# A two-layer hybrid decoder trunk on one core: mixer outputs and differential q and k turned on VectorE instead of TensorE, and weight high halves begun earlier

## The chip, the core and the metric

The kernel runs on one core of a Trainium2 chip. The core has TensorE (PE), VectorE (DVE), ScalarE (ACT), GpSimd (POOL) and SyncE (SP), each with its own queue of instructions, and DMA queues. SBUF is the core's memory of 128 partitions, PSUM holds matmul outputs in banks of 128 x 512 float32. The metric is the device time of one execution in microseconds (us).

## The reference

x (512 tokens x 2048, float32) goes through two layers:

```python
h = rms_norm(x, norm_g)
p = h @ w_in                       # 2048 x 7192: all projections at once
ya = gla_mixer(aq, ak, av, alr, ...)  * silu(az)      # gated linear attention
yb = swa_mixer(bq, bk, bv, ...)       * silu(bz)      # sliding window 128, sinks
yc = diff_mixer(cq, ck, cv, ...)      * silu(cz)      # differential attention
yd = gdn_mixer(dqkv, dbeta, da, ...)  * silu(dz)      # gated DeltaNet
x  = x + concat([ya, yb, yc, yd]) @ w_out             # 2048 x 2048
```

Each mixer has 4 heads, each 128 wide. In the differential mixer a head's q and k are two halves of 64 columns; each half is normalised over its 64 columns and scaled by its gain (q also by 64 ** -0.5), two softmaxes over all earlier tokens are taken, and w = p1 - lambda * p2 is applied to v.

## The kernel before, in words

**Projections.** To keep float32 accuracy, every operand of a projection is split into a high half (rounded by the engine to the matmul's format) and a low half (the rest), and each product is three matmuls: hi x hi, hi x lo, lo x hi, in `project` (line 552). A projection step ("kt") takes 128 input rows to 512 columns: 4 PSUM banks x 3 = 12 matmuls of 128 x 512. A layer has 14 chunks of 512 output columns (dq, dk, dv, dz, bz, az, aq, av, bq, bkv, cq, ck, cv, cz) x 16 steps, and the output projection of 4 x 12 + 4 x 4 steps: 288 steps, in 144 pairs of weights. The first 12 input rows of the output projection are the outputs of DeltaNet (chunks 0 to 3 of `y`), linear attention (4 to 7) and the window mixer (8 to 11); the last four steps of each output group wait for the differential mixer (12 to 15), which runs during the first 12.

**Weights.** SyncE loads each pair of weight steps raw (`w_raw`, 3 buffers). GpSimd issues a second load of the same pair into `w_hi` (3 buffers, line 484, `high_halves`), which arrives rounded, and makes `w_lo = w_raw - w_hi` (4 buffers, line 509), two subtractions a pair. It issues the load of pair g + 1 after the first subtraction of pair g; the issue waits until TensorE has used up pair g - 2. `kt_done` counts TensorE's steps.

**Mixers beside projections.** Each mixer is a generator of stages for TensorE; `project` hands one out after so many matmuls (its `stages`, `skip`, `spread`). The order on each engine is written out by hand, with counted semaphores (`Steps`) between engines. DeltaNet runs beside dz, bz, az, aq, av; linear attention tiles 0 to 3 beside bq, bkv, cq, ck; the window tiles 0 and 1 beside cv and 2 and 3 beside cz; the differential tiles 3, 2, 1, 0 beside the four output groups. All four mixers share the four PSUM banks `mix`.

**What the change touches.** The window tile `swa` has, between its scores (line 797) and the transposes of its probabilities (818), 8 transposes (807) that turn the differential q and k of that tile, normalised on VectorE (1886), into `mix`; ScalarE copies them back with their gains (1366). `turn_y` (953) turns each mixer's output, four 128 x 128 transposes a chunk: chunks 0 to 3 in front of the last step of cz, chunks 4 to 11 in pairs in front of the first four steps of the first output group, chunks 12 to 15 near the end. From `mix`, ScalarE makes the high half (`y_hi`, 1383) and VectorE the low half (`y_lo`, 1928). The scores of the differential mixer are at 843 (tiles 3 and 2) and 875 (tiles 1 and 0, two heads at once). In the linear attention VectorE turns q and k in blocks of 32 (1835, 1840), then waits for TensorE, copies under a mask (1844) and updates the state (1852, 1855), for which TensorE's output matmuls (749) wait. ScalarE asks for the residual (4 MB, line 1391) when the last window tile is done. `x_group` makes the low halves of the next layer's input and the sums of its squares, with `x_sums` (936, 938) on TensorE in front of the last step of dq; `lambda_sums` and `lambdas` prepare parameters.

Of the kernel before, what the change touches and what calls it, by code (L numbers as in the profile page):

```python
# [7 lines left out]
F32 = mybir.dt.float32  # L8
# [7 lines left out]
P = 128  # L16
# [3 lines left out]
GW = 512  # L20
# [27 lines left out]
SLOT = dict(dq=4, dk=5, dv=8, dz=3, bz=4, az=5, aq=6, av=7, bq=8, bkv=9, cq=10, ck=11, cv=12, cz=13)  # L48
# [118 lines left out]
PREP_PE = "q k".split()  # L167
PREP_ACT = "qT kT".split()
# [46 lines left out]
def hybrid_trunk(nc, x, wstream, wsmall, pcol, prow, wlr, cf, masks, out, rows):  # L215
    ctx = ExitStack()
    with ctx:
# [68 lines left out]
        def cols(ap, n=128, parts=P):  # L286
# [35 lines left out]
              for i in range(2)]  # L322
# [12 lines left out]
                 PT=s7[:, 1024:2048].rearrange("p (h c) -> p h c", h=HEADS))  # L335
        RQ = general[:, :, :].rearrange("p a (g c) -> p (a g) c", c=DK)
        f3 = [slot(3)[:, i] for i in range(4)]
        Z = dict(S=((f3[0], f3[1]), (f3[2], f3[3])), WT=(unit(4, 0), unit(4, 1)), OS=unit(4, 2), SQO=unit(4, 3),
                 GATE=unit(5, 0))
# [3 lines left out]
        cden = stat[:, 52:60]  # L343
        ssb, rsb = stat[:, 64:70], stat[:, 72:78]
# [14 lines left out]
        rows_out, rows_in = sem("rows_out"), sem("rows_in")  # L359
        kt_done = sem("kt_done")  # L360
        acc_ready, acc_free = sem("acc_ready"), sem("acc_free")
        xres_in, xout = sem("xres_in"), sem("xout")
        lam_steps = sem("lam_steps")
        lam_act = sem("lam_act")
# [21 lines left out]
        def lay(prefix, *parts):  # L386
# [4 lines left out]
        X_DVE = Steps(sem("x_dve"), [s for n in T for s in [f"lo{4*n+i}" for i in range(4)] + [f"pair{n}"] +  # L391
                                     ([f"four{n}"] if n else []) + [f"g{n}"]])
        S_PE = Steps(sem("setup_pe"), ["rsum", "small", "ba", "dec"] + [f"yT{k}" for k in range(KT)])
# [19 lines left out]
        R_PE = Steps(sem("prep_pe"), names("", T, PREP_PE))  # L413
        R_ACT = Steps(sem("prep_act"), names("", T, PREP_ACT))
# [44 lines left out]
        def _(pool):  # L459
# [27 lines left out]
            for l in range(DEPTH):  # L487
                for i in range(PAIRS):
# [5 lines left out]

                    pool.wait_ge(raw_in[g % RAW], g // RAW * 16 + 16)
                    if g >= FIRST_HI:
                        pool.wait_ge(hi_in[g % HI], len(range(FIRST_HI + (g - FIRST_HI) % HI, g + 1, HI)) * 16)
                    for k in range(2):
# [12 lines left out]
                        if k == 0 and FIRST_HI <= g + 1 < DEPTH * PAIRS:  # L511
                            high_halves(g + 1)
# [3 lines left out]
        def _(pe):  # L516
# [244 lines left out]
            def swa(l, t):  # L761
# [50 lines left out]
                pe.wait_ge(R_ACT.sem, R_ACT.at(l, f"{t}.kT"))  # L812
# [14 lines left out]
            def dif(l, t):  # L827

                n = t + 1
                qT, kT, v = (slot(SLOT[c]) for c in ("cq", "ck", "cv"))  # L830

                def scores(h):
# [33 lines left out]
                def pair_scores(g):  # L866
# [5 lines left out]
                    for h in (2 * g, 2 * g + 1):  # L872
                        for m in range(2):
                            r = slice(DK * m, DK * m + DK)
                            last = nc.tensor.matmul(mix[m][:, 256 * (h % 2):256 * (h % 2) + P * n],  # L875
                                                    qT[r, t, HD * h:HD * h + HD], kT[r, 0:n, HD * h:HD * h + HD],
# [64 lines left out]
            def turn_y(l, k):  # L941

                src = slot(SLOT[("dz", "az", "bz", "cz")[k // 4]])
                if k == 0:

                    pe.wait_ge(B_DVE.sem, B_DVE.at(l, f"{TILES-1}.y3"))
                    pe.wait_ge(R_ACT.sem, R_ACT.at(l, f"{TILES-1}.kT"))
                elif k == 3 * HEADS:
                    pe.wait_ge(C_DVE.sem, C_DVE.at(l, "0.y3"))
                elif k >= 4:  # L950
                    pe.wait_ge(S_DVE.sem, S_DVE.at(l, f"ylo{k-4}"))
# [5 lines left out]
            for l in range(DEPTH):  # L957
# [50 lines left out]
                for i in range(2):  # L1008
# [3 lines left out]
                    def y_first(k, l=l):  # L1012
# [1107 lines left out]
```

## Time and profile before

| | |
|---|---|
| median of 3 runs (lowest, highest) | 1816.85 us (1816.59, 1820.76) |
| the profiled execution: its time, its span | 1817.91 us, 1816.1 us |
| granted clock of TensorE | 1.0 of full speed |
| TensorE busy | 1806.1 us, 99% |
| GpSimd, VectorE, ScalarE busy | 920.1, 854.8, 505.0 us |
| DMA | 324.99 MB, mean 179 GB/s |
| w_raw, w_hi loads of 512 KB, issue to landing (median) | 4.5 us, 3.8 us |
| TensorE's waits by name, whole span | w_lo 2.6 us, issue 1.2, others 3.0 |

A matmul's recorded duration is longer than its step: matmuls follow each other before the one in front has drained, so their durations overlap, and TensorE's cost of something is read from the distance between starts. A group of instructions of one line is merged to one row with a count. "Idle" in brackets is the time in which the engine had nothing in flight before that instruction, and who ended it. Fp32 matmuls that aren't transposes have two records each.

### The profile page before, as it was taken

Reading aid. Unit: us, or ns where it says so; the run is one execution under the profiler, and the core shown is the slowest. Engines: PE = TensorE matmul, PEld = TensorE weight load, DVE = VectorE, ACT = ScalarE, POOL = GpSimd, SP = SyncE. Lnnn points to the kernel's source line nnn. Section 1 sums busy time; section 2 is a strip of 40 time slices with the busy share of each in tenths; the row PEclk is TensorE's granted clock in tenths of the full one; section 3 lists DMA queues with packets and bytes.
Section 4 is the critical chain, followed back from the end, with each engine's and each line's share of the span. In section 5 each row is a group of like instructions: output and inputs, shape, how many; then the busy total and the mean of one; then the engine's idle time right before and its main releaser. Section 6 shows DMA issues by size and latency. Waiting matters only on the chain. (4 is left out here: it accounts for less than half of the span.)

```text
span 1816.1 us, 23463 instructions
## 1 busy us (share of the span) xinstructions
PE 1806.1 (99%) x9382; PEld 1484.4 (82%) x9382; DVE 854.8 (47%) x1829; ACT 505.0 (28%) x967; POOL 920.1 (51%) x864
## 2 busy tenths in 40 slices
PE   9999999999999999999999999999999999999999
PEld 7788888888888888788877888888888878877887
DVE  7546815523333443544534478264333344445342
ACT  6213114022222543322312131141222235433220
POOL 5555544545555444445465555445455454444454
PEclk9999999999999999999999999999999999999999
DMA  7566545645555547456765665555555565474556
GB/s 273 169 186 208 175 152 160 186 143 183 177 175 181 163 140 243 129 161 185 233 213 181 191 203 176 158 155 171 162 178 177 169 184 156 148 242 134 160 170 209
DMA packets 94508, 324.99 MB, mean 179 GB/s; under 512 B 10144, under 2 KB 10688, under 8 KB 94144
## 3 DMA queue, kind: packets, MB, share of 16 engines
q1 hardware_dynamic: 43904, 155.73, 27.8%
q0 software_dynamic: 40320, 146.82, 26.7%
q10 hardware_dynamic: 10176, 20.94, 3.2%
q8 instruction: 74, 1.21, 0.3%
q14 instruction: 34, 0.28, 0.0%
HBM read 315.05 MB, written 8.40 MB: 178 GB/s over the span
## 5 line engine op out<-in xcount | busy, mean ns | idle before, releaser
L509 POOL TENSOR_TENSOR w_lo<-w_raw,w_hi 128x512 fp32r<-128x512 f32 x575 | 759.5, 1321 | 650.3 <-DMA w_hi<-in_wstream 488.4
L552 PE MATMUL acc<-w_hi,actT_hi 128*128 128x512 f32 x1408 | 559.8, 398 | 0.0
L552 PE MATMUL acc<-w_hi,actT_lo 128*128 128x512 f32 x1408 | 548.9, 390 | 0.0
L552 PE MATMUL acc<-w_lo,actT_hi 128*128 128x512 f32 x1408 | 548.5, 390 | 0.0
L552 PE MATMUL acc<-actT_hi,w_hi 128*128 128x512 f32 x896 | 358.4, 400 | 4.3 <-POOL w_lo L509 2.6
L552 PE MATMUL acc<-actT_hi,w_lo 128*128 128x512 f32 x896 | 349.6, 390 | 0.0
L552 PE MATMUL acc<-actT_lo,w_hi 128*128 128x512 f32 x896 | 349.2, 390 | 0.0
L552 PEld LDWEIGHTS acc<-w_hi,actT_lo 128*128 128x128 f32 x1408 | 264.3, 188 | 55.9
L552 PEld LDWEIGHTS acc<-w_hi,actT_hi 128*128 128x128 f32 x1408 | 264.5, 188 | 55.1 <-issue 2.8
L552 PEld LDWEIGHTS acc<-w_lo,actT_hi 128*128 128x128 f32 x1408 | 264.7, 188 | 51.7
L484 POOL DMA_DIRECT2D w_hi<-in_wstream x280 | 159.8, 571 | 234.6 <-PE acc L552 230.3
L552 PEld LDWEIGHTS acc<-actT_hi,w_hi 128*128 128x128 f32 x896 | 168.3, 188 | 54.1 <-issue 19.8
L552 PEld LDWEIGHTS acc<-actT_hi,w_lo 128*128 128x128 f32 x896 | 168.2, 188 | 35.9
L552 PEld LDWEIGHTS acc<-actT_lo,w_hi 128*128 128x128 f32 x896 | 168.5, 188 | 32.7 <-issue 0.5
L1579 DVE SCALAR_TENSOR_TENSOR slots<-slots,pcol_all 128x511 f32<-128x511 f32 (+2 forms) x72 | 86.6, 1208 | 1.7
L1052 ACT ACTIVATE slots<-acc,xr 128x512 f32<-128x512 f32 x56 | 37.9, 690 | 167.8 <-PE acc L552 167.8
L1937 DVE TENSOR_TENSOR slots<-acc,slots 128x512 f32<-128x512 f32 x64 | 43.1, 690 | 88.0 <-PE acc L552 88.0
L1560 DVE TENSOR_TENSOR slots<-acc,slots 128x512 f32<-128x512 f32 x24 | 15.7, 689 | 129.0 <-PE acc L552 91.8
L1818 DVE SCALAR_TENSOR_TENSOR slots<-mix,slots 128x256 f32<-128x256 f32 x8 | 3.4, 425 | 133.3 <-ACT slots L1294 133.3
L601 PEld LDWEIGHTS mix<-slots 128*128 128x128 f32 x400 | 48.5, 191 | 2.0
L601 PE MATMUL mix<-slots 128*128 128x128 f32 x400 | 49.0, 275 | 0.0
L1928 DVE SCALAR_TENSOR_TENSOR actT_lo<-mix,pcol_all,actT_hi 128x512 fp32r<-128x512 f32 x32 | 22.4, 746 | 42.1 <-ACT actT_hi L1383 42.1
(264 smaller groups left out, 1586.2 us busy)
## 6 DMA issues: line engine op xcount, KB each, us to landing
w_raw<-in_wstream SPq DMA_DIRECT2D x288, 512.0 KB, 4.5
w_hi<-in_wstream POOLq DMA_DIRECT2D x280, 512.0 KB, 3.8
out_x<-slots ACTq DMA_DIRECT2D x7, 1024.0 KB, 7.1
slots<-in_x ACTq DMA_DIRECT2D x1, 4096.0 KB, 19.5
slots<-out_x ACTq DMA_DIRECT2D x1, 4096.0 KB, 19.2
slots<-in_x SPq DMA_DIRECT2D x3, 1024.0 KB, 12.0
slots<-rows ACTq DMA_DIRECT2D x2, 1024.0 KB, 5.7
out_x<-slots ACTq DMA_DIRECT2D x4, 256.0 KB, 2.1
```

Source lines behind the costliest of these rows:

```text
L484: pool.dma_start(w_hi[:, g % HI].rearrange("p a n -> p (a n)"), wstream[g:g + 1].rearrange("a p n -> p (a n)")).then_inc(hi_in[g % HI], 16)
L509: pool.tensor_tensor(w_lo[:, n % RING], w_raw[:, g % RAW, k], w_hi[:, g % HI, k].bitcast(F32), ALU.subtract).then_inc(w_ready, 1)
L552: last = nc.tensor.matmul(acc[b][:, :], lhsT, rhs, start=(k == 0 and i == 0), stop=(k == kts - 1 and i == 2))
L601: last = nc.tensor.matmul(mh[bank][:, h], lhsT[:, h], rhs[:, h], start=True, stop=True)
L1052: nc.scalar.activation(slot(SLOT[c])[:, b], acc[b][:, :], ACT.Copy, scale=r) \
L1560: dve.tensor_tensor(slot(SLOT[c])[:, b], acc[b][:, :], rrow, ALU.mult).then_inc(acc_free, 1)
L1579: dve.scalar_tensor_tensor(dst[:, d:], src[:, 0:SEQ - d], tap[i], dst[:, d:], ALU.mult, ALU.add).then_inc(CONV_DVE.sem, CONV_DVE.one(f"{c} ...
L1818: dve.scalar_tensor_tensor(V["G"], mix[1][:, 0:256], 0.0, V["T0"], ALU.min, ALU.subtract) \
L1928: dve.scalar_tensor_tensor(actT_lo[:, k], mix[k % 4][:, :], pcv(l, PC["y"] + k), actT_hi[:, k].bitcast(F32), ALU.mult, ALU.subtract) \
L1937: dve.tensor_tensor(xs, acc[b][:, :], xs, ALU.add).then_inc(acc_free, 1)
```

## The change

Mixer outputs: the outputs of DeltaNet (dz) and linear attention (az) are turned into slots of their own on VectorE, in blocks of 32 x 32 (`turn_blocks`, 16 instructions each), dz during the linear attention's tiles 0 and 1, az during the window tiles. `turn_y` keeps chunks 8 to 15; 8 to 11 are turned together in front of the third step of the first output group. `y_hi` and `y_lo` of chunks 0 to 7 read the turned slots.

Differential q and k: VectorE turns each tile's q and k within the four blocks of 32 partitions (`turn_c`, 8 instructions a tile), ScalarE's queue writes the four pieces to DRAM and reads them back with the blocks in their places (`hop_back`, 8 DMAs a tile), and ScalarE scales q once for all (gain of q x gain of k x 64 ** -0.5). The scores read q with a column step of 4 numbers and k in runs of 32.

Weights: in the first 8 and the last 8 pairs of a layer GpSimd issues the next pair's high halves before it waits for this pair's.

Order: the residual is asked for after cz is taken out of PSUM; the input's low halves 12 to 15 come before the third sum of squares; the taps are halved first of all, and the lambda sums come after the convolution of dq in layer 0; the differential scores' buffer is slot 10 in place of 3, cq is in slot 3, cz in 5.

```diff
-SLOT = dict(dq=4, dk=5, dv=8, dz=3, bz=4, az=5, aq=6, av=7, bq=8, bkv=9, cq=10, ck=11, cv=12, cz=13)
+SLOT = dict(dq=4, dk=5, dv=8, dz=3, bz=4, az=5, aq=6, av=7, bq=8, bkv=9, cq=3, ck=11, cv=12, cz=5)
+Y_TURNED = dict(dz=10, az=13)
...
+        turned_piece = dict(q0=smT[:, 0:256], q1=smT[:, 256:512], k0=wlr_sb[:, :], k1=s6[:, 768:1024])
...
@@ GpSimd, for each pair i of a layer (g over both layers)
+                    follows = FIRST_HI <= g + 1 < DEPTH * PAIRS
+                    dense_only = i < KT // 2 or i >= PAIRS - LAST_KTS // 2
+                    if follows and dense_only:
+                        high_halves(g + 1)
                     pool.wait_ge(raw_in[g % RAW], g // RAW * 16 + 16)
...
-                        if k == 0 and FIRST_HI <= g + 1 < DEPTH * PAIRS:
+                        if k == 0 and follows and not dense_only:
                             high_halves(g + 1)
@@ TensorE, sliding-window tile
-                pe.wait_ge(N_DVE.sem, N_DVE.at(l, f"{t}.ck"))
-                for i, c in enumerate(("cq", "ck")):
-                    for h in H:
-                        last = nc.tensor.transpose(mh[i][:, h], slot(SLOT[c])[:, t, h * HD:h * HD + HD], ident)
-                    last.then_inc(R_PE.sem, R_PE.one(f"{t}.{'qk'[i]}"))
                 yield
                 yield
-                pe.wait_ge(R_ACT.sem, R_ACT.at(l, f"{t}.kT"))
+                pe.wait_ge(B_ACT.sem, B_ACT.at(l, f"{t}.kT"))
@@ TensorE, differential scores (the paired scores of tiles 1 and 0 alike)
+                qT = slot(SLOT["cq"]).rearrange("p t (c h) -> p t h c", h=HEADS)
+                kT = slot(SLOT["ck"]).rearrange("p t (b h c) -> p t b h c", b=P // BLK, h=HEADS)
...
                         pe.wait_ge(S_DVE.sem, S_DVE.at(l, f"ylo{3*HEADS-1}"))
+                        pe.wait_ge(hop_in, 128 * TILES * (l + 1))
+                        pe.wait_ge(Q_ACT.sem, Q_ACT.at(l, f"q{TILES-1}"))
...
-                        last = nc.tensor.matmul(mix[m][:, 0:P * n], qT[r, t, HD * h:HD * h + HD],
-                                                kT[r, 0:n, HD * h:HD * h + HD], start=True, stop=True)
+                        last = nc.tensor.matmul(mix[m][:, 0:P * n], qT[r, t, h],
+                                                kT[r, 0:n, :, h].rearrange("p t b c -> p (t b) c"),
+                                                start=True, stop=True)
@@ TensorE, outputs turned
-                    def y_first(k, l=l):
-                        if k == KT - 1:
-                            for m in range(4):
-                                turn_y(l, m)
...
-                            for m in (4 + 2 * k, 5 + 2 * k):
-                                if m < 3 * HEADS:
+                            if k == 2:
+                                for m in range(2 * HEADS, 3 * HEADS):
                                     turn_y(l, m)
@@ ScalarE
+                    if CHUNKS[8 + t] == "cq":
+                        act.wait_ge(Y_DVE.sem, Y_DVE.at(l, f"dz{P//BLK-1}{P//BLK-1}"))
                     take_out(l, CHUNKS[8 + t])
...
+                def hop_back(t):
+                    act.wait_ge(hop_out, 64 * (TILES * l + t + 1))
+                    for i, c in enumerate(("cq", "ck")):
+                        for r in range(P // BLK):
+                            act.dma_start(slot(SLOT[c])[BLK * r:BLK * r + BLK, t].rearrange("p (b c) -> p b c", b=P // BLK),
+                                          hops[l, i, :, t, P * r:P * r + P].rearrange("(b p) c -> p b c", b=P // BLK)) \
+                                .then_inc(hop_in, 16)
...
+                    if t:
+                        hop_back(t - 1)
+                    for i, p in enumerate(TURNED):
+                        act.wait_ge(T_DVE.sem, T_DVE.at(l, f"{t}.{p}"))
+                        act.dma_start(hops[l, i // 2, :, t, 256 * (i % 2):256 * (i % 2) + 256], turned_piece[p]) \
+                            .then_inc(hop_out, 16)
                     w(B_DVE, "nm")
...
-                    for i, c in enumerate(("q", "k")):
-                        w(R_PE, c)
-                        g = PC[f"g{c}_c"]
-                        nc.scalar.activation(slot(SLOT["c" + c])[:, t], mix[i][:, :], ACT.Copy,
-                                             scale=pcv(l, g)).then_inc(R_ACT.sem, R_ACT.one(f"{t}.{c}T"))
...
+                hop_back(TILES - 1)
+                for k in range(2 * HEADS):
+                    y_hi(k)
+                take_out(l, "cz")
                 act.wait_ge(B_DVE.sem, B_DVE.at(l, f"{TILES-1}.y3"))
...
                 act.dma_start(xT, (out if l else x).rearrange("(k p) n -> p k n", p=P)).then_inc(xres_in, 16)
-                for k in range(4):
-                    y_hi(k)
-                take_out(l, "cz")
-                for k in range(4, 12):
-                    y_hi(k)
+                act.wait_ge(hop_in, 128 * TILES * (l + 1))
+                for t in T:
+                    nc.scalar.activation(slot(SLOT["cq"])[:, t], slot(SLOT["cq"])[:, t], ACT.Copy,
+                                         scale=pcv(l, PC["gq_c"])).then_inc(Q_ACT.sem, Q_ACT.one(f"q{t}"))
+                for k in range(2 * HEADS, 3 * HEADS):
+                    y_hi(k)
@@ VectorE
+                def turn_blocks(c, rows):
+                    src = slot(SLOT[c]).rearrange("p t (h c) -> p t h c", h=HEADS)
+                    dst = slot(Y_TURNED[c]).rearrange("p h (t c) -> p t h c", t=TILES)
+                    for r in rows:
+                        rs_ = slice(BLK * r, BLK * r + BLK)
+                        for f in range(P // BLK):
+                            fs = slice(BLK * f, BLK * f + BLK)
+                            dve.transpose(dst[fs, :, :, rs_], src[rs_, :, :, fs]) \
+                                .then_inc(Y_DVE.sem, Y_DVE.one(f"{c}{r}{f}"))
...
+                    if t < 2:
+                        turn_blocks("dz", [2 * t])
                     w(A_PE, "a")
...
                     gate(A_DVE, l, t, gz, V["GATE"])
+                    if t < 2:
+                        turn_blocks("dz", [2 * t + 1])
...
+                def turn_c(t, pieces):
+                    for p in pieces:
+                        i = TURNED.index(p)
+                        c, half_ = ("cq", "ck")[i // 2], 2 * (i % 2)
+                        v = slot(SLOT[c])[:, t].rearrange("p (h r c) -> p h r c", h=HEADS, r=P // BLK)
...
+                        if TILES * l + t:
+                            dve.wait_ge(hop_out, 64 * (TILES * l + t))
+                        for r in range(2):
+                            o = turned_piece[p][:, P * r:P * r + P].rearrange(
+                                "p (h c) -> p h c" if c == "ck" else "p (c h) -> p h c", h=HEADS)
+                            last = dve.transpose(o, v[:, :, half_ + r])
+                        last.then_inc(T_DVE.sem, T_DVE.one(f"{t}.{p}"))
                 sums(0)
                 normalise(0)
+                turn_c(0, TURNED[:2])
                 for t in T:
...
+                    turn_c(t, TURNED[2:])
...
                     gate(B_DVE, l, t, gz, W["GATE"])
+                    turn_blocks("az", [t])
...
                         normalise(t + 1)
+                        turn_c(t + 1, TURNED[:2])
+                    if t == TILES - 1:
+                        for k in range(HEADS):
+                            y_lo(k)
                     w(B_PE, "pv")
...
-                for k in range(12):
+                dve.wait_ge(hop_out, 64 * TILES * (l + 1))
+                dve.memset(smT[:, :], 1.0).then_inc(ones_done, 1)
+                for k in range(HEADS, 3 * HEADS):
                     y_lo(k)
```

## Rows read from the trace of the kernel before

**Rows 1.** Page, busy time of each engine, share of the span, instructions.

```profile
PE 1806.1 (99%) x9382; PEld 1484.4 (82%) x9382; DVE 854.8 (47%) x1829; ACT 505.0 (28%) x967; POOL 920.1 (51%) x864
```

**Rows 2.** Timeline of TensorE (start, duration, group, count), around a window tile's transposes.

```profile
603.81 0.39 PE L552 MATMUL acc<-w_hi,actT_lo 128*128 128x512 f32 x1
...
605.85 0.40 PE L552 MATMUL acc<-w_hi,actT_lo 128*128 128x512 f32 x1
606.08 1.04 PE L807 MATMUL mix<-cf_sb,slots 128*128 128x128 f32 x8
606.88 0.47 PE L552 MATMUL acc<-w_hi,actT_hi 128*128 128x512 f32 x1
607.19 0.39 PE L552 MATMUL acc<-w_lo,actT_hi 128*128 128x512 f32 x1
```

**Rows 3.** TensorE's groups by form (busy us, mean ns, idle before): both transpose lines.

```profile
L953 PE MATMUL mix<-cf_sb,slots 128*128 128x128 f32 x128 | 16.3, 272 | 0.0
...
L807 PE MATMUL mix<-cf_sb,slots 128*128 128x128 f32 x64 | 8.3, 272 | 0.0
```

**Rows 4.** Timeline of TensorE in front of the last input step.

```profile
695.53 0.40 PE L552 MATMUL acc<-w_hi,actT_lo 128*128 128x512 f32 x1
...
697.75 0.39 PE L552 MATMUL acc<-w_lo,actT_hi 128*128 128x512 f32 x1
```

**Rows 5.** Timeline of TensorE at the layer boundary, matmuls that waited (idle in brackets).

```profile
908.43 0.47 PE L552 MATMUL acc<-actT_hi,w_hi 128*128 128x512 f32 x1 [0.66 <-issue]
...
915.13 0.47 PE L552 MATMUL acc<-actT_hi,w_hi 128*128 128x512 f32 x1 [1.01 <-POOL w_lo L509]
...
922.43 0.47 PE L552 MATMUL acc<-actT_hi,w_hi 128*128 128x512 f32 x1 [1.58 <-POOL w_lo L509]
```

**Rows 6.** Timeline of GpSimd at the layer boundary.

```profile
908.27 0.57 POOL L484 DMA_DIRECT2D w_hi<-in_wstream  x1
...
913.41 1.57 POOL L509 TENSOR_TENSOR w_lo<-w_raw,w_hi 128x512 fp32r<-128x512 f32 x1 [3.24 <-issue]
```

**Rows 7.** Busy us by engine, clock, DMA share, GB/s, 910 to 920 us.

```profile
910.00:920.00 10.00, 8.99 (x40) 7.12 (x39) 9.93 (x12) 4.94 (x8) 3.96 (x5) 1.00 0.95 342
```

**Rows 8.** VectorE's groups by form: two turns in blocks of 32.

```profile
L1835 DVE STREAM_TRANSPOSE slots<-slots 32x128 f32<-32x128 f32 x128 | 38.7, 303 | 4.0
...
L1758 DVE STREAM_TRANSPOSE slots<-slots 32x256 f32<-32x256 f32 x16 | 7.0, 436 | 0.5
```

**Rows 9.** Busy us by engine, 624 to 644 us (window tiles).

```profile
624.00:644.00 20.00, 20.00 (x105) 16.98 (x104) 10.00 (x18) 10.54 (x23) 9.53 (x9) 1.00 0.54 163
```

**Rows 10.** Timelines of ScalarE, TensorE and GpSimd, window tiles and after.

```profile
629.61 1.24 ACT L1366 ACTIVATE slots<-mix,pcol_all 128x512 f32<-128x512 f32 x2
...
633.44 1.03 PE L818 MATMUL mix<-cf_sb,slots 128*128 128x128 f32 x8
...
681.45 0.60 ACT L1371 ACTIVATE slots<-mix 128x512 f32<-128x512 f32 x1 [2.39 <-PE mix L818]
...
703.75 1.28 POOL L509 TENSOR_TENSOR w_lo<-w_raw,w_hi 128x512 fp32r<-128x512 f32 x1 [8.35 <-DMA w_hi<-in_wstream]
```

**Rows 11.** Timeline of ScalarE's queue, a DMA issue.

```profile
9.80 0.52 ACTq L1125 DMA_DIRECT2D slots<-in_prow  x1
```

**Rows 12.** Timelines of VectorE and TensorE, linear attention, tile 0.

```profile
425.62 0.78 DVE L1844 COPY_PREDICATED general<-mask_sb,mix 128x256 f32<-128x256 uint8 x2 [1.14 <-PE mix L734]
...
427.95 1.39 DVE L1855 TENSOR_SCALAR slots<-slots 128x128 f32<-128x128 f32 x2
...
431.39 1.06 PE L749 MATMUL mix<-slots,general 128*128 128x128 f32 x8
```

**Rows 13.** Weight loads by form: the scores of tiles 1 and 0.

```profile
L875 PEld LDWEIGHTS mix<-slots 64*128 64x128 f32 x64 | 4.8, 186 | 3.0 <-issue 2.1 <-DVE stat L1971 0.7
```

**Rows 14.** Timelines of TensorE, scores of tile 3 and of tile 0.

```profile
716.22 1.13 PE L843 MATMUL mix<-slots 64*128 64x512 f32 x4
...
827.85 0.71 PE L875 MATMUL mix<-slots 64*128 64x128 f32 x8
```

More of the change, by code:

```diff
@@ L212, in dif_dve, with hybrid_trunk @@
     return out + [f"0.{x}" for x in "redo y0 y1 y2 y3".split()]
-def hybrid_trunk(nc, x, wstream, wsmall, pcol, prow, wlr, cf, masks, out, rows):
+def hybrid_trunk(nc, x, wstream, wsmall, pcol, prow, wlr, cf, masks, out, rows, hops):
     ctx = ExitStack()
@@ L390, in hybrid_trunk @@
         X_ACT = Steps(sem("x_act"), [f"{s}{k}" for k in range(KT) for s in ("hi", "sq")])
-        X_DVE = Steps(sem("x_dve"), [s for n in T for s in [f"lo{4*n+i}" for i in range(4)] + [f"pair{n}"] +
-                                     ([f"four{n}"] if n else []) + [f"g{n}"]])
-        S_PE = Steps(sem("setup_pe"), ["rsum", "small", "ba", "dec"] + [f"yT{k}" for k in range(KT)])
+        X_DVE = Steps(sem("x_dve"), [s for n in range(2) for s in [f"lo{4*n+i}" for i in range(4)] + [f"pair{n}"] +
+                                     ([f"four{n}"] if n else []) + [f"g{n}"]] +
+                      [f"lo{k}" for k in range(8, 12)] + ["pair2"] + [f"lo{k}" for k in range(12, 16)] +
+                      ["four2", "g2", "pair3", "four3", "g3"])
+        S_PE = Steps(sem("setup_pe"), ["rsum", "small", "ba", "dec"] + [f"yT{k}" for k in range(2 * HEADS, KT)])
+        Y_DVE = Steps(sem("y_turned"), [f"{c}{r}{f}" for c in Y_TURNED for r in range(P // BLK) for f in range(P // BLK)])
         S_ACT = Steps(sem("setup_act"), ["lnr", "lnx", "rrow", "xr", "half", "ba", "eb", "aab", "ea", "la", "A", "L", "LT", "decs"] +
@@ L1308, in _, with y_hi @@
                     nc.scalar.activation(sa, sa, ACT.Exp, scale=-0.5).then_inc(*s("ro"))
+                    if CHUNKS[8 + t] == "cq":
+                        act.wait_ge(Y_DVE.sem, Y_DVE.at(l, f"dz{P//BLK-1}{P//BLK-1}"))
                     take_out(l, CHUNKS[8 + t])
+                def y_hi(k):
+                    if k < 12:
+                        act.wait_ge(kt_done, kt_value(l, IN_KTS - KT + k))
+                    if k < 2 * HEADS:
+                        c = ("dz", "az")[k // HEADS]
+                        act.wait_ge(Y_DVE.sem, Y_DVE.at(l, f"{c}{P//BLK-1}{P//BLK-1}"))
+                        src = slot(Y_TURNED[c])[:, k % HEADS]
+                    else:
+                        act.wait_ge(S_PE.sem, S_PE.at(l, f"yT{k}"))
+                        src = mix[k % 4][:, :]
+                    nc.scalar.activation(actT_hi[:, k], src, ACT.Copy, scale=pcv(l, PC["y"] + k)) \
+                        .then_inc(S_ACT.sem, S_ACT.one(f"yhi{k}"))
                 def squares(t):
@@ L1500, in lambdas @@
                                   .broadcast_to([P, DEPTH, 4]), ALU.mult).then_inc(lam_steps, 1)
[L1501 to L1503 removed]
+                dve.wait_ge(lam_steps, 2 * DEPTH + 5)
             def x_lo(l, k):
@@ L1519, in x_group, with x_pairs, x_total @@
                             .then_inc(w_ready, 1)
+            def x_pairs(l, n):
+                a = 4 * (n % 2)
                 dve.wait_ge(X_ACT.sem, X_ACT.at(l, f"sq{4*n+3}"))
+                dve.tensor_tensor(sq[:, a:a + 2], sq[:, a:a + 2], sq[:, a + 2:a + 4], ALU.add) \
+                    .then_inc(X_DVE.sem, X_DVE.one(f"pair{n}"))
+            def x_total(l, n):
                 a = 4 * (n % 2)
                 s = lambda step: (X_DVE.sem, X_DVE.one(f"{step}{n}"))
-                dve.tensor_tensor(sq[:, a:a + 2], sq[:, a:a + 2], sq[:, a + 2:a + 4], ALU.add).then_inc(*s("pair"))
                 dve.wait_ge(X_DVE.sem, X_DVE.at(l, f"pair{n}"))
@@ L1537, in gate, with x_group @@
                 dve.scalar_tensor_tensor(Zs, tmp, 1.0, Zs, ALU.add, ALU.mult).then_inc(St.sem, St.one(f"{t}.g3"))
+            def x_group(l, n):
+                x_low_halves(l, n)
+                x_pairs(l, n)
+                x_total(l, n)
             dve.wait_ge(norm_in, 16)
-            for n in range(3):
+            taps = pcol_all[:, :, PC["conv"]:]
+            dve.tensor_scalar(taps, taps, 0.5, None, ALU.mult).then_inc(taps_halved, 1)
+            for n in range(2):
                 x_group(0, n)
-            lambda_sums()
+            x_low_halves(0, 2)
+            x_pairs(0, 2)
             for l in range(DEPTH):
@@ L2036, in _ @@
                     add(18 + n, n, IN_KTS + OUT_KTS + 4 * n + 3)
-                    if l + 1 < DEPTH and n:
+                    if l + 1 < DEPTH and 0 < n < 3:
                         x_group(l + 1, n - 1)
+                if l + 1 < DEPTH:
+                    x_low_halves(l + 1, 2)
+                    x_pairs(l + 1, 2)
 def constants():
```

90 lines of the change are left out of this document (47 added, 43 removed).

## The prediction

> **What bounds the kernel now.** I read the page's busy shares first: TensorE is busy in 1806.1 of 1816.1 us, and no other engine is above 51% [rows 1]. Then the PE timeline. Plain projection matmuls start 0.2267 us apart (nine steps from 603.81 to 605.85) [rows 2]. There are 2 layers x 288 steps x 12 = 6912 of them, 1567 us of the span. All that shortens the kernel is what stands between them: about 249 us of small matmuls and true waits. A step on VectorE, ScalarE or a DMA queue counts only if TensorE comes to wait for it. In the timeline of the whole span the starts of neighbouring projection matmuls lie further apart for want of something in four places only, and three of them are at the layer boundary [rows 5].
>
> **Part 1, transposes taken off TensorE.** In each tile of the sliding-window mixer the 8 transposes of differential q and k go. Around one such group the projection matmuls start at 605.85 and 607.19, two steps apart [rows 2]: 1.34 - 2 x 0.2267 = 0.89 us for 8, 0.11 each (the mean duration of 272 ns overlaps). 4 tiles x 2 layers x 0.89 = 7.1 us, and the 64 records say the same number of groups [rows 3]. Of the 16 output transposes groups (4 transposes each) a layer, those of chunks 0 to 7 go, 32 transposes a layer, half of the 128 [rows 3]. The group of 16 in front of the last input step goes whole: 697.75 - 695.53 - 0.45 = 1.77 us [rows 4]. Chunks 4 to 11 came in four groups of 8 (0.89 each, as above, 3.55 us), and 8 to 11 now come as one group of 16 (1.77). Per layer 1.77 + 3.55 - 1.77 = 3.55, for two 7.1 us. **Sum of part 1: -14.2 us**, all of it on TensorE's own line, so all of it counts, if nothing takes its place.
>
> **Part 2, high halves begun early.** At the layer boundary TensorE waited three times on w_lo. The idle shown is 0.66, 1.01 and 1.58 us; a gap is that plus the modelled 0.39, less the step of 0.2267, so 0.82, 1.17 and 1.74, and each restart costs another 0.08 (the next start is 0.31 on, as at 607.19 [rows 2]): 3.97 us [rows 5]. GpSimd's line shows why: the high half issued at 908.27 is used at 913.41, 5.1 us on, behind a subtraction of 1.3 and an issue of 0.57, in a loop that must turn in 2 x 12 x 0.2267 = 5.44 us [rows 6]. In the first 8 and last 8 pairs of a layer the next high half is now issued before the wait for this one. The semaphore wait that it carries (kt_done 2g+2) holds back the first subtraction of the pair by one step of 2.7 us, but its result is wanted two steps (5.4 us) later and takes 1.3. Issue and landing then overlap the other pair, and the loop is 3.2 us of GpSimd. The DMA engines are 95% busy there and move 342 GB/s [rows 7], 1.9 MB in 5.44 us, and a pair wants 1.0 MB of that. I take **-3.9 us** of 3.97 (bounds 0, where the transfers' rate and not their start was the limit, and -4.0). In layer 0's start and at the end no wait was recorded that it could remove.
>
> **Part 3, the new load on VectorE.** Turning dz and az: 16 + 16 instructions a layer of 32 x 512. Rows show 303 ns for 128 and 436 for 256 elements [rows 8], 133 ns per 128, so 0.70 us each: 64 x 0.70 = 45 us. Turning q and k: 8 a tile of 128 x 128, 64 x 0.30 = 19 us. VectorE goes from 47% to about 50%; only places count. In the sliding-window tiles 4 turns (2.8 us) come before the copy that waits for the probabilities' transposes at 633.44 [rows 10]; in 624 to 644 VectorE is busy 10.0 of 20 us [rows 9]: covered. In the gated linear attention (tiles 0 and 1 of each layer) 4 turns stand in front of the masked copy. There VectorE idled 1.14 us, so 1.7 us remain: its last scaling, now 427.95 + 1.39 = 429.34, becomes 431.0, and TensorE takes it up at 431.39 [rows 12]. Cover left: 0.4 us in each of 4 places. Bounds: 0 and 4 x 1.5 (each turn twice as long, less the cover, would be 2.4); I take **+0.4 us**, since in rows 8 such turns cost what their size says.
>
> **Part 4, the hop.** ScalarE's queue issues 4 DMAs out and 8 back per tile. The nearest row has 0.52 us for an issue [rows 11], 12 x 0.5 = 6 us of sequencer in a tile of 22, while ScalarE is 10.5 of 20 busy [rows 9] and loses two copies, 1.24 us together [rows 10]. Queued behind the wait for the turned pieces are the four exponentials, on which TensorE's transposes at 633.44 hang; the exponentials ended at 629.61 [rows 10], so there are 3.8 us, and the pieces are turned before the scores. Cost nothing; without that cover what is over 3.8 us would fall on TensorE 8 times. The last hop back is issued behind the last tile's copy (681.45 + 0.60 [rows 10]) by 686; the eight high halves after it need 8 x 0.62 = 5 us and end by 691, and the last input step begins at 697 [rows 4]. Its data (0.5 MB, 5 us as in rows 6) are wanted in the fifth step of the output projection, 13 us after that. VectorE's four low halves of dz now stand ahead of the last tile's outputs, near 689, and their next user comes after 697. The 4 MB of the residual are now asked for at about 700 in place of 690. Before, GpSimd waited 8.35 us for a high half behind them [rows 10] and TensorE did not; the half has four steps (10.9 us) and now 16 transposes and two score groups (4.3 us) as cover: nothing. The hop's 8.4 MB (2.6% of the kernel's 325) find the engines 54% busy [rows 9]: nothing. Lambdas, taps and the sums of squares in another order: TensorE has no wait in front of them; nothing.
>
> **Part 5, the scores' operands.** q comes back with the token's column step 4 numbers (16 bytes) and is the stationary operand of all score matmuls. 64 weight loads in the two early tiles [rows 13] and 64 in the two late ones read it. No load of the trace has such a step, so bounds: below 0 (a load hidden behind the 512 columns before it; nothing makes it faster), above a doubling. A load with its transpose passes in 0.11 us, so a load asks at most 0.11 and a doubling adds as much. Those of the two late tiles (4 in 1.13 us, 0.26 each) hide even 0.22; those of the two early tiles (8 in 0.71, 0.09 each) don't [rows 14]: 64 x 0.11 = +7.1 us. Rows 13 (186 ns a load, about that of the plain ones) are nearest to the lower end, I take **+2 us**. k comes in runs of 32 numbers as moving operand: 0.
> The Trainium skill, page "SBUF — State Buffer", section "Door 1: The DMA port swizzle", speaks against this edit: consecutive accesses to one line of 16 bytes run at full rate, and each access that crosses into a new line pays. By its lines each of q's numbers would now lie in a line of its own, which is the first rival below; without the rule the term would be 0 and the time 2 us less.
>
> **Sum.** The profiled execution took 1817.91 us (span 1816.1 and 1.8 around it). -14.2 - 3.9 + 0.4 + 2 = -15.7, so a span of 1800.4 and an execution of 1802.2. The median of the runs is 1816.85, 1.1 below the profiled one, which gives **1801.2 us**.
>
> **Rivals.**
> (a) Other side: the strided weight loads. If a load takes four times as long (one number used of the four that lie together), 0.44 us stand against 0.26 in the late tiles and 0.09 in the early ones: 64 x 0.18 + 64 x 0.35 = 34 us, and 1816.85 - 17.7 + 34 = 1833. It decides from about 0.14 us more per load (17.7/128). For it: nothing in the trace has this step. Against: the loads have 0.26 us each in half of the cases. Chance 5%. The doubling (+7.1 in place of 2) gives 1806: 10%.
> The skill's rule above would have (a) come out; no row bears on it.
> (b) Nothing gained at the boundary, because DMA is the limit there (95% busy [rows 7]): +3.9, 1805. Against: the chain of GpSimd alone explains the gaps, and a queue that starts earlier also ends earlier. 13%.
> (c) A new wait for VectorE in the linear attention and the window tiles: its turns at 1.0 us in place of 0.70 put 1.2 us on each of 4 places, less 0.4, and up to 0.5 on 8 tiles: +3 + 4, 1808. 10%.
> (d) ScalarE's queue or the hop late: issues of 1 us would make 12 us a tile, 2 to 3 us past the cover on each of 8 tiles, about +20: 1821, or the first scores wait for the hop. Against: no issue above 0.52. 6%.
> (e) The forecast: 56%.
>
> **Range and chances.** What a measurement of this kernel can tell from no change is 0.3%, 5.4 us. (e), (b), (c) and the doubling are all below 1811.4: 56 + 13 + 10 + 10 = 89%, of which I give 5 to mixtures that end within 0.3%, and 2 of (d)'s 6 end there too. Faster 0.84, same 0.07, slower 0.09 (5 of (a), 4 of (d)). The likeliest case alone has 1797 (no cost in parts 3 to 5, a little more from fewer restarts) to 1804; with (b) and (c) the range is 1797 to 1810.
>
> **What would show it.** Groups of 8 transposes in front of the probabilities' transposes and 64 fewer of the output transposes; neighbouring projection matmuls 0.23 apart over the whole layer boundary; no idle of TensorE named after VectorE's turns, the hop or w_lo; the score groups as long as before (1.13 us for 4, 0.71 for 8). A longer score group shows (a), TensorE idle before the linear attention's value matmuls shows (c), idle before the probabilities' transposes or the first scores (d). A span above 1806 would make the prediction wrong in its mechanism.

## The result and the profile after

The changed kernel takes **1804.14 us** (median, 1803.79 to 1805.92), the kernel before beside it 1816.72 (1815.61 to 1820.76): ratio 0.9924, 95% interval 0.991 to 0.9937. The forecast was 1801.2. The profiled execution took 1804.25 us with a span of 1802.5, so the span is 13.6 us shorter; the prediction's sum was 15.7. It had taken 1.1 us off for the distance between profiled run and median, which is 0.1 us in the changed kernel.

The page's busy shares; against [rows 1] TensorE has 128 records fewer and VectorE 130 more:

```profile
PE 1795.4 (100%) x9254; PEld 1478.6 (82%) x9254; DVE 917.9 (51%) x1959; ACT 501.3 (28%) x959; POOL 920.8 (51%) x864
```

Groups by form (busy us, mean ns). Of the two transpose lines of [rows 3] one is left, with half its records. The turns on VectorE cost what [rows 8] said by size (0.70 us for 32x512); the last two differ in one thing, q's is written with a step of four numbers:

```profile
L963 PE MATMUL mix<-cf_sb,slots 128*128 128x128 f32 x64 | 8.0, 273 | 0.0
...
L1874 DVE STREAM_TRANSPOSE slots<-slots 32x512 f32<-32x512 f32 x64 | 45.0, 703 | 1.9
L1975 DVE STREAM_TRANSPOSE smT<-slots 128x128 f32<-128x128 f32 x32 | 8.8, 388 | 0.0
L1975 DVE STREAM_TRANSPOSE wlr_sb<-slots 128x128 f32<-128x128 f32 x16 | 3.9, 277 | 0.0
```

The weight loads of the scores, tiles 3 and 2 in the first row, tiles 1 and 0 in the second. The kernel before had 184 ns (third row) and 186 ns [rows 13]:

```profile
L853 PEld LDWEIGHTS mix<-slots 64*128 64x128 f32 x64 | 8.7, 316 | 3.8 <-issue 1.4 <-DVE slots L2094 0.7 <-DVE stat L2098 0.7
L886 PEld LDWEIGHTS mix<-slots 64*128 64x128 f32 x64 | 8.1, 321 | 2.8 <-issue 2.1 <-DVE stat L2064 0.7
...
L843 PEld LDWEIGHTS mix<-slots 64*128 64x128 f32 x64 | 4.8, 184 | 3.8 <-issue 2.1 <-DVE slots L2001 0.7
```

And TensorE's timeline in tile 3 and tile 0, 1.13 and 0.71 us before [rows 14]:

```profile
708.79 1.25 PE L853 MATMUL mix<-slots 64*128 64x512 f32 x4
...
821.86 1.20 PE L886 MATMUL mix<-slots 64*128 64x128 f32 x8
```

At the layer boundary one of the waits of [rows 5] is left, a small one, and for another reason (VectorE frees the bank late). GpSimd now issues the next high half in front of its two subtractions, which was [rows 6] the other way round:

```profile
903.14 0.47 PE L563 MATMUL acc<-actT_hi,w_hi 128*128 128x512 f32 x1 [0.39 <-DVE slots L2028]
```
```profile
897.61 0.57 POOL L491 DMA_DIRECT2D w_hi<-in_wstream  x1 [2.30 <-DMA w_hi<-in_wstream]
898.72 3.12 POOL L520 TENSOR_TENSOR w_lo<-w_raw,w_hi 128x512 fp32r<-128x512 f32 x2 [0.54 <-issue]
903.05 0.57 POOL L491 DMA_DIRECT2D w_hi<-in_wstream  x1 [1.21 <-DMA w_hi<-in_wstream]
```

**Where the time went, stage by stage.** Both kernels have the same 6912 projection matmuls in the same order. Taking the start of the first one of each stage from TensorE's timeline, before and after, gives how much shorter each stage became. "After" is the changed kernel, the last two columns are experiments told of below. Stages not shown changed by under 0.1 us, but for waits of 0.2 to 1.3 us around the start of layer 1's ck (TensorE waiting there for the linear attention's halves), which come and go by the run.

```
stage (us, both layers alike within 0.06)   after   plain q   turns made twice
bq, bkv (linear attention tiles 0, 1)        0.0      0.0      +2.4, +3.9
cv (two window tiles' transposes)           -1.8     -1.8      -1.8
cz (two more, the 16, first 8 of outputs)   -4.4     -4.4      -4.4
out0 (other outputs' transp.; scores 3)     -0.5     -1.1      -0.5
out1 (scores tile 2)                        +0.5      0.0      +0.5
out2 (scores tile 1)                        +0.4      0.0      +0.4
out3 (scores tile 0)                        +1.0      0.0      +1.0
layer boundary (once)                       -3.4     -3.8      -4.1
```

The very first stage (the start of layer 0) differs between the profiled runs by up to 3 us even for one and the same kernel (two profiles of the changed one), so it is left out of all readings. TensorE waits there for VectorE's sums and low halves: 0.82 us at 48.37 us in the first profile, 1.53 us at 49.39 in the second, and in the second the granted clock was then 0.76, 0.50 and 0.89 in the windows from 50 to 56 us.

### The profile page after: what moved, and what is told of

Its sections match the earlier page's. It is cut to its first block, busy times and chain, and to the rows that moved or that the text cites. A ratio compares the mean times of both kernels' runs of the same rounds, so it can differ in the third digit from the quotient of the medians.

```text
span 1802.5 us, 23457 instructions
## 1 busy us (share of the span) xinstructions
PE 1795.4 (100%) x9254; PEld 1478.6 (82%) x9254; DVE 917.9 (51%) x1959; ACT 501.3 (28%) x959; POOL 920.8 (51%) x864
## 4 chain that ended last, share of the span: by engine, by line
PE 95%; DVE 3%; DMA 1%; ACT 1%; issue 0%; SPq 0%; ACTq 0%
PE acc L563 84%; PE mix L612 2%; PE mix L853 1%; DVE actT_lo L1536 1%; DMA w_raw<-in_wstream 1%; PE mix L783 1%; PE mix L873 1%; PE mix L808 1%; PE mix L606 1%; PE mix L886 1%; DVE slots L2028 0%; PE mix L760 0%; PE mix L982 0%; PE mix L963 0%; DVE slots L1564 0%; DMA slots<-in_x 0%
## 5 line engine op out<-in xcount | busy, mean ns | idle before, releaser
L1606 DVE TENSOR_TENSOR slots<-acc,slots 128x512 f32<-128x512 f32 x24 | 15.7, 688 | 125.0 <-PE acc L563 91.8
L1874 DVE STREAM_TRANSPOSE slots<-slots 32x512 f32<-32x512 f32 x64 | 45.0, 703 | 1.9
```

The costliest lines, as they stand in the source:

```text
L1874: dve.transpose(dst[fs, :, :, rs_], src[rs_, :, :, fs]) \
```

## Experiments

**Plain q.** My theory was that the step of 16 bytes in q's weight loads holds the missing 2 us and more. The edit writes q plainly and lets ScalarE's scaling, which exists anyway, put each head's columns side by side in a place of its own.

```diff
-                qT = slot(SLOT["cq"]).rearrange("p t (c h) -> p t h c", h=HEADS)
+                qT = q_home(t).rearrange("p (h c) -> p h c", h=HEADS)
...
-                                "p (h c) -> p h c" if c == "ck" else "p (c h) -> p h c", h=HEADS)
+                                "p (h c) -> p h c", h=HEADS)
...
-                for t in T:
-                    nc.scalar.activation(slot(SLOT["cq"])[:, t], slot(SLOT["cq"])[:, t], ACT.Copy,
...
+                for t in reversed(T):
...
+                    nc.scalar.activation(
+                        q_home(t).rearrange("p (h b c) -> p h b c", h=HEADS, b=P // BLK),
+                        slot(SLOT["cq"])[:, t].rearrange("p (b h c) -> p h b c", h=HEADS, b=P // BLK),
...
```

> The changed kernel, with q of the differential mixer laid so that the 128 columns of one head's weights stand side by side again (VectorE turns it plainly, and ScalarE's scaling moves it to its place), the rest as it is. My theory: the 2 us that are missing from the forecast are q's weight loads at a step of 16 bytes, whose mean went from 184 to 316 ns; the projection matmuls around the four late tiles start 0.38 + 0.47 + 0.43 + 0.97 us later per layer than the transposes' saving says, so undoing the step gives back 2 x 2.25 = 4.5 us: 1799.6 us, with the loads back at some 185 ns and the 64x512 score matmuls from 10.0 back to 9.0 us per 32. Rival: k, whose moving operand is now read in runs of 32, slows the score matmuls, and then this changes under 0.5 us.

Measured: 1799.73 us (1799.16 to 1801.49), ratio to before 0.9897 [0.9881, 0.9913]. The loads and TensorE's groups of the two kinds of tile are back where they were, though k is still read in runs of 32:

```profile
L854 PEld LDWEIGHTS mix<-slots 64*128 64x128 f32 x32 | 2.4, 184 | 1.9 <-issue 1.4
L887 PEld LDWEIGHTS mix<-slots 64*128 64x128 f32 x64 | 4.8, 186 | 3.0 <-issue 2.1 <-DVE stat L2069 0.7
```
```profile
709.11 1.13 PE L854 MATMUL mix<-slots,general 64*128 64x512 f32 x4
...
820.70 0.71 PE L887 MATMUL mix<-slots 64*128 64x128 f32 x8
```

By the stages, with one more digit than the table has, the step costs (0.56 + 0.48 + 0.44 + 0.97) x 2 = 4.9 us, by the medians 4.4. The rival (k's runs) falls.

**The step alone, in the kernel before,** where no hop and no turn on VectorE is in play: 16 bytes, then 8.

```diff
+                            dst, src = dst.rearrange("p (c h) -> p h c", h=HEADS), mh[i]
...
-                        last = nc.tensor.matmul(mix[m][:, 0:P * n], qT[r, t, HD * h:HD * h + HD],
+                        last = nc.tensor.matmul(mix[m][:, 0:P * n], qT[r, t, h],
```

> The kernel before, with one thing of the change: ScalarE stores the turned q with the four heads interleaved, so that TensorE loads each head's 128 weight columns at a step of 16 bytes. No hop, no turn on VectorE, k stays plain. My theory: weight loads of 316 ns in place of 184, and the whole +4.5 us: 1821.2. Rival (the step is free and the hop or k's runs of 32 cost the 4.5 us): 1816.7.

> The kernel before with q stored two heads interleaved: a step of 8 bytes. If the load's time grows evenly with the step (184 at 4 bytes, 316 at 16), it is 228 ns here and costs a third: +1.5 us, 1818.2. If it is the larger of a fixed time and the step's, it may be free: 184 ns and 1816.7. [...]

Measured: 16 bytes 1824.66 us against 1817.58 of before on that chip, ratio 1.004 [1.0025, 1.0054]; 8 bytes 1817.46, ratio 0.9997 [0.9987, 1.0007]. The 7.1 us are more than 4.5, but the output stages grew by 0.49, 0.47, 0.36 and 0.97 us in each layer, 4.6 in all. In the profiled run the first stage is 4.5 us longer too, with a wait of 3.37 us for VectorE's low halves; the edit touches nothing there. That the other 2.5 us of the medians are of this kind is likely and not shown; 4.6 is at the lower end of what the interval allows (4.5 to 9.8). The loads of tiles 3 and 2 with 16 bytes, and with 8:

```profile
L844 PEld LDWEIGHTS mix<-slots 64*128 64x128 f32 x64 | 8.7, 316 | 3.8 <-issue 1.4 <-DVE stat L2009 0.7 <-DVE slots L2005 0.7
```
```profile
L844 PEld LDWEIGHTS mix<-slots 64*128 64x128 f32 x64 | 5.0, 192 | 3.8 <-issue 2.1 <-DVE slots L2006 0.7
```

184, 192 and 316 ns at 4, 8 and 16 bytes: not even growth (228 was expected for that), but next to nothing up to 8 bytes. The Trainium skill ("SBUF — State Buffer", section "Door 1: The DMA port swizzle") says that SBUF lies in lines of 16 bytes, that full rate wants at least two accesses in a row on a line, and that an access which crosses to a new one pays. At 8 bytes two numbers in a row lie on a line, at 16 bytes one. The trace agrees with the condition of two: 4% more and 72% more. The page gives no price, and a price paid at each new line alone would have shown at 8 bytes too.

**TensorE makes q's and k's transposes too**, at their old place, unused:

```diff
+                pe.wait_ge(N_DVE.sem, N_DVE.at(l, f"{t}.ck"))
+                for i, c in enumerate(("cq", "ck")):
+                    for h in H:
+                        nc.tensor.transpose(mh[i][:, h], slot(SLOT[c])[:, t, h * HD:h * HD + HD], ident)
```

> The changed kernel, in which TensorE also makes the eight transposes of q and k in each window tile that the change took from it, at their old place; what they give isn't used. My theory: they cost their own time and no wait, 0.89 us per group of eight, 8 groups, +7.1 us: 1811.3. Rival: what was gained there was the wait for ScalarE's copies out of PSUM (which doesn't come back here), and this costs much less than 7 us.

Measured: 1811.94 us (1809.47 to 1814.65), ratio 0.9966 [0.9955, 0.9977], 7.8 above the changed kernel. In the stages cv and cz 1.8 us come back each, 7.2 in all. For q and k the gain of part 1 is TensorE's own time, 0.9 us for each group of eight; no wait was in it. For the outputs no run puts the transposes back; there the stages alone show the gain.

**Without the early high halves.**

```diff
-                    dense_only = i < KT // 2 or i >= PAIRS - LAST_KTS // 2
+                    dense_only = False
```

> The changed kernel with the high halves of the weights begun where they were before (after the first matmuls of a pair, everywhere), the rest as it is. My theory: the early issue is worth the 3.4 us that the matmuls at the layer boundary come earlier: 1807.5 us, with three waits of PE for the low halves (0.7, 1.0 and 1.6 us) back at 905 to 925 us. Rival: those waits went because VectorE's order at the boundary was changed in the same edit, and then it stays at 1804.

Measured: 1808.29 us (1806.83 to 1813.25), ratio 0.9947 [0.993, 0.9964]. The boundary's stages are then 0.7 us shorter than before in place of 3.4 to 4.1, so the early issue is worth 2.7 to 3.4 us. Waits like those of [rows 5] are back, shorter ones and one more:

```profile
898.30 0.50 PE L563 MATMUL acc<-actT_hi,w_hi 128*128 128x512 f32 x1 [0.44 <-POOL w_lo L520]
904.37 0.47 PE L563 MATMUL acc<-actT_hi,w_hi 128*128 128x512 f32 x1 [0.33 <-issue]
911.07 0.47 PE L563 MATMUL acc<-actT_hi,w_hi 128*128 128x512 f32 x1 [0.98 <-POOL w_lo L520]
917.27 0.47 PE L563 MATMUL acc<-actT_hi,w_hi 128*128 128x512 f32 x1 [0.48 <-POOL w_lo L520]
```

**Another order at the boundary, against the one wait left.**

```diff
-                        x_group(l + 1, n - 1)
+                        x_low_halves(l + 1, n - 1)
+                        x_pairs(l + 1, n - 1)
```
(and the totals behind the next four additions)

> The changed kernel with the boundary's order alone: the total over a group's squares moved behind the next four additions. One wait is left at the boundary (903.14 us, 0.39 us idle), for a PSUM bank that VectorE frees late since it still does the squares' sums. My theory: the order takes 0.4 to 0.6 us away: 1803.6. Rival: the low halves take 1.23 us each there instead of 1.05 whatever the order (VectorE and GpSimd at once), something else is then as late, and nothing changes: 1804.1.

> The changed kernel once more, unchanged, for comparison with those that run on the same chip. 1804.1 us. In the first profile the high halves' issue at the boundary (the last 16 k-tiles of layer 0 and the first 16 of layer 1) was worth 3.4 us, in three other kernels that share that code 4.1; I expect either, by the run, and not a third value.

Measured: the order 1804.44 us, ratio 0.9921 [0.9907, 0.9935]; the changed kernel again 1804.67, ratio 0.993 [0.9919, 0.9942]. A miss: the wait at 903.14 is gone with the new order, but it is also gone in the second profile of the unedited kernel, whose boundary is 4.1 us shorter than before. The wait was one run's, and this order is worth nothing that these runs can tell.

**The hop's way out doubled.**

```diff
+                        for home in (spare, hops):
+                            act.dma_start(home[l, i // 2, :, t, 256 * (i % 2):256 * (i % 2) + 256], turned_piece[p]) \
```

> The changed kernel in which every turned piece of q and k is also sent to a second DRAM tensor that nobody reads, and the buffer isn't written again before both have landed: 64 DMA issues more on ScalarE's queue, of 0.5 us each at the most, and 4 MB more. My theory: the hop and its issues lie beside TensorE's projection matmuls, with 3.8 us of cover in a window tile, so 2.1 us more in each is hidden: 1804.1. Rival: ScalarE's queue is near the path in the window tiles, and the issues show with up to 8 x 2.1 = 17 us.

Measured: 1804.02 us (1803.56 to 1804.08), ratio 0.9924 [0.9912, 0.9936]: nothing. In the window tiles from 620 to 640 us (busy us of PE, PEld, DVE, ACT, POOL, then clock, DMA share, GB/s) the DMA engines are 70% busy in the changed kernel and 78% here, and TensorE is busy all the time. The row is this run's:

```profile
620.00:640.00 20.00, 20.00 (x94) 16.75 (x93) 15.86 (x29) 10.77 (x25) 8.40 (x9) 1.00 0.78 224
```

**Where VectorE's cover ends.** Ahead of the masked copy in the linear attention four turns were added. These kernels do one, two, or all four of them twice.

```diff
                     if t < 2:
+                        turn_blocks("dz", [2 * t], again=1)
                         turn_blocks("dz", [2 * t])
```

> The changed kernel with the first four of VectorE's 0.70 us turns in each of the GLA mixer's first two tiles done twice (the second writes the same again). They stand ahead of the copy that TensorE waits for; by the trace that wait has 0.9 us of cover. My theory: 2.8 us more of which 0.9 is hidden, in four places: +7.7 us, 1811.8. Rival: VectorE is not near the path there, as the unchanged time of this stage says: under 1 us.

> The changed kernel with one of the 0.70 us turns ahead of the GLA mixer's masked copy done twice, in four places. All four done twice made TensorE wait 2.1 us for 2.9 us added, so the cover is 0.75 us. My theory: 0.72 us more is just hidden: TensorE's wait under 0.1 us in each place, total 0 to +0.4: 1804.3. Rival: there is no such cover (the wait grows with every turn and the 2.9 to 2.1 comes from elsewhere): 0.5 us or more in each place, +2 us and above.

> The same with two of the four turns done twice. My theory: 1.44 - 0.75 = 0.7 us of wait and some 0.25 us beside it in four places, +2.8 to +3.8 us: 1807.5. With all four done twice, the clock granted to TensorE also fell to 0.50 for 3 us after the second tile's wait of 2.1 us (and not after the first's), worth 1.6 us each time. If a wait of 2.1 us is what makes it fall, it stays at 1.00 here; if any wait in that tile does, it falls here too: +6 us, 1810.

Measured: all four twice 1817.71 us (ratio 1.0005 [0.9995, 1.0014], the whole gain of the change gone), one twice 1808.62 (0.9954 [0.9941, 0.9968]), two twice 1810.04 (0.9958 [0.9947, 0.997]). Three times the same theory, three times too low: +7.7, +0.2 and about +3 expected, +13.6, +4.5 and +5.9 measured; the stages of the linear attention grew by 12.6, 5.2 and 5.7. Two things were not in it. The first explains the runs with one and two turns twice, the second most of what the run with all four has beyond its forecast.

First, VectorE's and GpSimd's lines in the changed kernel and then with one turn twice:

```profile
429.83 0.48 DVE L1921 TENSOR_SCALAR slots<-slots 128x128 f32<-128x128 f32 x2
...
430.93 1.29 POOL L520 TENSOR_TENSOR w_lo<-w_raw,w_hi 128x512 fp32r<-128x512 f32 x1
...
431.24 1.06 PE L760 MATMUL mix<-slots,general 128*128 128x128 f32 x8
```
```profile
430.48 1.93 DVE L1928 TENSOR_SCALAR slots<-slots 128x128 f32<-128x128 f32 x2
...
431.03 1.28 POOL L521 TENSOR_TENSOR w_lo<-w_raw,w_hi 128x512 fp32r<-128x512 f32 x1
...
432.45 1.16 PE L761 MATMUL mix<-slots,general 128*128 128x128 f32 x8 [0.96 <-DVE slots L1928]
```

The cover is there: the two scalings end at 430.31 and TensorE takes up their result at 431.24, 0.93 us later (0.92 to 1.03 in the four places). But the scalings, 0.65 us later, meet GpSimd's subtraction of 431.03 and last until it is done (432.31): 1.93 us for what took 0.48. A delay of 0.72 us became one of 2.1. With two turns twice the scalings take 1.42 us. With all four twice these last two scalings meet no subtraction and take 0.48 again. The turns themselves are not held up: that of 424.39 in the changed kernel took 0.70 us beside a subtraction of 424.43 to 425.72. The Trainium skill, page "SBUF — State Buffer", section "SBUF: two separate sides", says that VectorE and GpSimd share one pair of ports, that VectorE takes it for operations in a mode that uses two ports or has two inputs in SBUF, and that whoever starts first has it for the whole instruction. The trace agrees in part. Whenever a scaling is held, it ends 0.1 us after the subtraction. But the scaling held here was recorded to start 0.35 us before the subtraction (0.52 in the second place) and lost 1.44 us (1.62) to one of 1.28. That it came second isn't what the records say, so how it is held stays open; no run here settles it.

Second, the clock. With all four twice TensorE sits idle 2.1 us in each place. After the second place of each layer the granted clock falls from 1.00 to 0.50, which is its lower level of 1.2 GHz. The rows are TensorE's timeline and the windows after it:

```profile
484.21 1.16 PE L761 MATMUL mix<-slots,general 128*128 128x128 f32 x8 [2.14 <-DVE slots L1928]
...
487.09 0.63 PE L564 MATMUL acc<-w_hi,actT_lo 128*128 128x512 f32 x1
487.52 0.63 PE L564 MATMUL acc<-w_hi,actT_hi 128*128 128x512 f32 x1
...
489.16 0.39 PE L564 MATMUL acc<-w_lo,actT_hi 128*128 128x512 f32 x1
```
```profile
486.00:488.00 2.00, 2.00 (x9) 1.54 (x6) 1.91 (x4) 1.80 (x3) 0.00 (x0) 0.50 0.19 76
488.00:490.00 2.00, 2.00 (x8) 1.65 (x7) 0.42 (x1) 1.67 (x3) 0.83 (x1) 0.73 0.00 0
```

The projection matmuls start 0.43 us apart for 3 us and not 0.23, which is the 1.6 us by which the growth of bkv (+3.93) exceeds that of bq (+2.37). After the equally long idle of the first place it stayed at 1.00, and with waits of 1.2 us (two turns twice) too; but in the first stage of the changed kernel's second profile it fell after an idle of 1.53 us. The length of the idle alone doesn't decide it, and what does stays open. Of the 5 us that were not expected with all four twice the clock has 3.1; the other 0.5 us in each place have no cause shown.

**The best version.** Plain q and the other order together:

> The changed kernel with plain q (as in the run before) and, at the layer boundary, the two sums of squares' totals put behind the next four additions to the residual on VectorE. Both edits together: 1804.1 - 4.5 - 0.5 = 1799.1 us, if each theory holds. Under the rivals of both, 1804.

Measured: 1799.51 us (1798.71 to 1801.0), ratio 0.9895 [0.9879, 0.9912], the same as plain q alone. Plain q is the edit to keep: 0.24% below the changed kernel.

## Why the prediction was nearly right

- **Part 1 (-14.2)** held. With plain q the stages cv, cz and out0 are 1.8 + 4.4 + 1.1 = 7.3 us shorter in each layer, 14.6 in all, and putting the half for q and k back cost 7.2. The reading of [rows 2] by distances of starts, not by the mean of 272 ns in [rows 3], was what gave 0.11 us a transpose: the mean would have made 17 us of the 7.1 for q and k.
- **Part 2 (-3.9)** held: 3.4 in the first profile, 3.8 and 4.1 in others. The 95% of [rows 7] was no limit (rival b). The early issue has 2.7 to 3.4 of it. The 0.7 us that stay without it may be the new order of VectorE's sums, which I had put at nothing; no run takes that order back alone.
- **Part 3 (+0.4)** measured 0.0: VectorE's scalings end 0.93 us before they are taken, not 0.4. The 1.39 us that [rows 12] showed for them before was itself a meeting with GpSimd (its subtraction began at 427.78, the scalings at 427.95), as in all four places before, and the turns moved them out of it. That the cover came out at twice the size foreseen was luck. The row of GpSimd before:

```profile
427.78 1.29 POOL L509 TENSOR_TENSOR w_lo<-w_raw,w_hi 128x512 fp32r<-128x512 f32 x1 [1.90 <-DMA w_hi<-in_wstream]
```

  So I had priced an instruction by a duration that held a collision. And the method, a cover in us against a delay in us, falls short here, as the three experiments show: rival (c) needed not turns of 1.0 us but one turn more, and pays 4.5 us. The upper bound was also worked out wrongly: turns twice as long cost 2.4 us in each place by the prediction's own terms, 9.6 and not 4 x 1.5, and the run with all four twice is that case and grew by 12.6.
- **Part 4 (0)** held, also with the way out doubled. The hop's 96 issues took 0.47 us each at the median and 0.49 in the mean; one took 1.55, three times what I had called the most, and it showed nowhere.
- **Part 5 (+2)** is the term that was mis-sized; it measured 4.9 by the stages, 4.4 by the medians. The step that failed is "Those of the two late tiles (...) hide even 0.22; those of the two early tiles (...) don't". Each load became 132 ns longer (bounds: 0 and a doubling; it is 1.7 times). Tile 0's group of eight paid 0.49 us, 61 ns a load. But tiles 3 and 2 paid as well, 0.12 us for each four (31 ns a load), although 0.26 us of matmul stood against each, and tile 1, which I had put with tile 0, paid 0.44 us for its 16, only 28 ns. A load that lies beside a long matmul is not free here. By the prediction's own signs the longer score groups (1.25 us for 1.13, 1.20 for 0.71) speak for rival (a), the strided loads, at 1.7 times and not at four. Had I taken the middle of my bounds (3.6) in place of the lower end's neighbourhood, the forecast would have been 1802.8. The measured time lies between the forecast and the doubling's 1806.

The sum by stages: -14.6 - 3.4 + 4.9 - 0.4 (the waits at ck and bq) = -13.5, and the span moved by -13.6. The forecast was -15.7: part 5 came out 2.9 us dearer and part 2 gave 0.5 less, while part 1, part 3 and the waits gave 0.4 more each. The median misses by 0.9 us more than the span, for the distance between profiled run and median named above.

## What to carry to other kernels

Where one engine is busy all the time, compare two versions by the starts of instructions that both have: most stages then reproduce to 0.05 us here, while medians move by 1 us, and nearly every term of a sum can be read alone. Look at the layout that a cheaper transpose leaves behind, for its reader pays: here the stationary operand could have a step of 8 bytes, not of 16. And cover on VectorE can end where GpSimd's next instruction begins, before the consumer needs the result.

## What the runs showed of the hardware

- A weight load of 64x128 fp32 takes 184 to 186 ns at a step of 4 bytes, 192 at 8, 316 to 321 at 16; of the 132 ns more, 28 to 35 ns show beside matmuls of 512 to 256 columns and 61 ns beside those of 128. A moving operand in runs of 32 numbers costs nothing (matmuls of 512 columns: mean 641 ns in the kernel before and with plain q).
- VectorE's turns in blocks of 32 write to a step of 16 bytes in 388 ns for 128x128, plainly in 264 to 277 (273 for the same q in the run with plain q).
- A scaling of 128x128 on VectorE takes 270 to 290 ns alone and up to 1906 ns beside a subtraction of GpSimd of 1.28 us; a turn of 32x512 takes its 0.70 us beside one.
- 0.7 us more work on VectorE in four places made the kernel 4.5 us slower; 2.9 us more made it 13.6 slower, of which 3.1 by the clock after two of four idles of 2.1 us. In another profile the clock fell after an idle of 1.5 us.
